# Ending a row norm inside the turn to columns: a product with a diagonal of reciprocal roots on top of a one-row product of the shift

## The chip, the cores and the metric

The kernel runs on one core of one Trainium2 chip. The metric is the device time of one execution in microseconds (us); three runs of the kernel before gave a median of 1448.42 us, with a lowest of 1444.13 and a highest of 1455.28. Names of engines: PE is TensorE, DVE is VectorE, ACT is ScalarE, POOL is GpSimd, SP is SyncE, which here only issues DMAs. PEld is the weight load of PE.

## The reference, cut to what matters

Two layers over 256 tokens of 1024 features, all float32. Layer 0 has two kinds of attention heads and a dense SwiGLU, layer 1 has differential attention and a SwiGLU of 8 experts, of which each token takes two. Every block ends in the same norm:

```
def layer_norm(x, g, b):
    mu = mean(x); var = mean((x - mu)**2)
    return (x - mu) * rsqrt(var + LN_EPS) * g + b

x = layer_norm(ALPHA * x + mixer(x),  ln1_g, ln1_b)
x = layer_norm(ALPHA * x + swiglu(x), ln2_g, ln2_b)

# layer 1, second block
logits = x @ w_router                 # 256 x 8
top_logit, top_e = top_k(logits, 2)
gate = softmax(top_logit)
out[t] = sum over the 2 chosen experts e of gate * swiglu(x[t], w_gate[e], w_up[e], w_down[e])
```

There are four norms: three of them feed products (before the dense SwiGLU, before layer 1, before the router and the experts), and the fourth gives the output.

## The kernel before

**Tiles.** The rows of x lie in two blocks of 128 tokens (`tb` 0 and 1) by 1024 features. Products need x with features on the partitions, so that each norm is followed by a turn: 8 pieces of 128x128 for each block, two banks of PSUM (the accumulation memory that PE writes) to a block, four pieces in each. ACT copies each bank to `xth` (rounded to the product's format), and DVE writes the rest, bank minus `xth`, to `xtl`. Each weight is split in the same way, by ACT to `whi` and by DVE to `wlo` (`split`, `hi`, `lo`), so a product is three products (lines 506, 507 and 508). The weights come as units of 1 MB. SP loads them in the order of use into slots of `raw`, 7 in the dense part and 14 with the experts, and each slot is loaded again once `wlo` of its unit is written (`lo_rdy`).

**Order.** There is no planner. Each engine's program is written out by hand, and semaphores join them. An expert has 42 units (`EXP_ORDER`): for each of 7 columns of hidden features two gate units, two up units, and then two down units of the column before. At unit j, ACT and DVE split unit j + 3, so that three units lie split ahead of PE.

**A norm** (`norm`, `norm_sum`, `norm_end` of DVE, `norm_root` of ACT, `turn` of PE). For each block DVE adds ALPHA times x and the branch's sum out of PSUM into `acc` (line 1384), takes the negated mean (1371), and writes (acc - mean) * gain to x (1395). Beside it, ACT squares with accumulation (995) and takes the root (990). DVE takes the reciprocal (1398) and ends the rows, x * reciprocal root + shift, in two halves (1400). PE turns the finished x by transposes against the identity (535, with the router 780), four to a bank. Between the blocks PE runs `keep_warm`, products of the identity with itself that nobody reads (513): 12 of them in the first two norms. ACT's copy is line 977, DVE's rest line 1259.

**The route.** After the third norm PE forms the router's logits from `xth` and `xtl` (768). DVE picks the two best experts of each token (lines 1512 to 1525), block after block. PE sums the choices into positions (799 to 805), and DVE makes the one-hot matrix `ohot_t` of the first expert (1534). The rows of the first expert are gathered by products with it (816), of `xrh` and `xrl`, the split of the finished x: ACT writes the one (1007), POOL the other (477). ACT also writes `acc`, ALPHA * x (1151), and zeroes `y` (1155).

**The last expert.** Before its first unit, DVE works out the gates and the rows of each token's two outputs (`gates_and_rows`, lines 1643 to 1663, each of these instructions waiting for the one before it). The outputs of all other experts lie in DRAM (`y_rows`). POOL gathers four blocks of 128 rows from there by indirect DMAs (485), and DVE adds them up with their gates (`picked_sum`, 1594) at the units in `PICK_AT`, (18, 23, 28, 33). The first sum waits for all four.

## Time and profile before

| | |
|---|---|
| three runs, us | 1444.13, 1448.42, 1455.28 (median 1448.42) |
| the profiled execution, us | 1446.74, of which span 1444.9 |
| busy in the span | PE 97%, PEld 84%, DVE 77%, ACT 65%, POOL 3% |
| PE's mean granted clock | 0.988 |
| a split of a unit | ACT 1.92, DVE 2.29 us |
| DVE in the slices of the dense SwiGLU (131 to 314 us) | busy 5 to 6 tenths |
| the three norms with a turn | about 118 to 131, 313 to 327, 441 to 454 us |
| the route | about 450 to 472 us |
| the experts | about 472 to 1431 us, one each 119.3 us; the last from 1306.6 us |

The span runs from the first to the last instruction. Matmuls overlap in the records, so that a busy PE may still be waiting for the array. A product of plain float32 operands shows as two records; a transpose, and a product in the rounded format, as one. The granted clock is given as a share of 2.4 GHz: 1.00 is that, 0.50 is 1.2 GHz.

### The profile page before, as it was taken

What the parts mean: (1) busy time and instruction counts of PE and PEld (TensorE: products, weight loads), DVE (VectorE), ACT (ScalarE), POOL (GpSimd) and SP (SyncE); (2) the same over time, 40 slices, a digit from 0 to 9 for tenths busy, and PEclk for the clock granted to TensorE, in tenths of its full rate; (3) what the DMA queues carried; (4) which work ended last, traced back from release to release, by engine and by line L of the source; (5) the groups of instructions that cost most, each with busy time, mean ns of one, the idle gap of its engine ahead of it and who ended that gap; (6) DMA issues with size and microseconds to landing.
All of it is one profiled execution on the core that took longest, in us unless ns stands there. A gap on an engine that the chain in (4) does not pass through costs nothing.

```text
span 1444.9 us, 19906 instructions
## 1 busy us (share of the span) xinstructions
PE 1405.6 (97%) x7580; PEld 1209.9 (84%) x7580; DVE 1118.8 (77%) x978; ACT 945.1 (65%) x838; POOL 41.0 (3%) x30
## 2 busy tenths in 40 slices
PE   8999999999988999999999999999999999998996
PEld 8988999989977888888888888888888888887885
DVE  4646454465566888888888988888888888888897
ACT  4655434445554777777777777777777777776775
POOL 1000000000001000000000000000000000002000
PEclk9999999999997999999999999999999999999998
DMA  9515555544136999999999999999999999998960
GB/s 362 222 64 203 191 185 181 199 146 175 60 161 251 413 384 369 366 402 370 342 411 383 374 364 389 389 357 392 368 357 405 376 367 378 392 372 334 421 235 31
DMA packets 62789, 438.59 MB, mean 304 GB/s; under 512 B 7096, under 2 KB 7120, under 8 KB 11152
## 3 DMA queue, kind: packets, MB, share of 16 engines
q1 hardware_dynamic: 59904, 425.75, 76.7%
q0 software_dynamic: 2688, 11.85, 2.3%
q8 instruction: 36, 0.59, 0.2%
q10 hardware_dynamic: 144, 0.27, 0.1%
q14 instruction: 17, 0.14, 0.0%
HBM read 431.54 MB, written 6.30 MB: 303 GB/s over the span
## 4 chain that ended last, share of the span: by engine, by line
PE 91%; DVE 5%; ACT 2%; issue 1%; DMA 1%; SPq 0%; DVEq 0%; ACTq 0%
PE ps L506 29%; PE ps L508 28%; PE ps L507 28%; PE ps L878 2%; ACT raw L1014 1%; DMA raw<-w_dense 1%; DVE raw L1271 1%; PE ps L664 1%; PE ps L612 1%; DVE acc L1384 1%; ACT biasb L995 1%; DVE wlo L1243 0%; PE ps L836 0%; DVE x L1400 0%; DVE raw L1312 0%
## 5 line engine op out<-in xcount | busy, mean ns | idle before, releaser
L1243 DVE TENSOR_TENSOR wlo<-raw,whi 128x2048 fp32r<-128x2048 f32 x398 | 910.2, 2291 | 207.2 <-ACT whi L962 205.5
L962 ACT ACTIVATE whi<-raw 128x2048 fp32r<-128x2048 f32 x398 | 762.2, 1918 | 273.1 <-PE ps L508 270.4
L506 PE MATMUL ps<-whi,xth 128*128 128x512 f32 (+1 forms) x1144 | 441.5, 386 | 7.5 <-DVE wlo L1243 3.8
L508 PE MATMUL ps<-whi,xtl 128*128 128x512 f32 (+1 forms) x1144 | 434.7, 380 | 0.0
L507 PE MATMUL ps<-wlo,xth 128*128 128x512 f32 (+1 forms) x1144 | 434.4, 380 | 0.0
L506 PEld LDWEIGHTS ps<-whi,xth 128*128 128x128 f32 x1144 | 215.6, 188 | 50.8 <-DVE wlo L1243 6.9
L508 PEld LDWEIGHTS ps<-whi,xtl 128*128 128x128 f32 x1144 | 215.6, 188 | 41.4
L507 PEld LDWEIGHTS ps<-wlo,xth 128*128 128x128 f32 x1144 | 215.9, 189 | 38.6
L506 PE MATMUL ps<-whi,hth 128*128 128x512 f32 x464 | 182.5, 393 | 0.0
L508 PE MATMUL ps<-whi,htl 128*128 128x512 f32 x464 | 180.8, 390 | 0.0
L507 PE MATMUL ps<-wlo,hth 128*128 128x512 f32 x464 | 180.7, 389 | 0.0
L506 PE MATMUL ps<-xth,whi 128*128 128x256 f32 x592 | 169.6, 287 | 3.6 <-issue 3.6
L507 PE MATMUL ps<-xtl,whi 128*128 128x256 f32 x592 | 168.9, 285 | 0.0
L508 PE MATMUL ps<-xth,wlo 128*128 128x256 f32 x592 | 168.8, 285 | 0.0
L506 PEld LDWEIGHTS ps<-xth,whi 128*128 128x128 f32 x592 | 115.0, 194 | 5.1 <-issue 4.5
L507 PEld LDWEIGHTS ps<-xtl,whi 128*128 128x128 f32 x592 | 115.0, 194 | 0.3
L508 PEld LDWEIGHTS ps<-xth,wlo 128*128 128x128 f32 x592 | 115.0, 194 | 0.0
L508 PEld LDWEIGHTS ps<-whi,htl 128*128 128x128 f32 x464 | 87.1, 188 | 18.6
L506 PEld LDWEIGHTS ps<-whi,hth 128*128 128x128 f32 x464 | 87.2, 188 | 18.0 <-issue 0.3
L507 PEld LDWEIGHTS ps<-wlo,hth 128*128 128x128 f32 x464 | 87.2, 188 | 17.3
L471 POOL DMA_INDIRECT biasb<-x_rows,slot_tok x7 | 19.2, 2741 | 744.2 <-DVE slot_tok L1621 744.2
L1582 DVE TENSOR_TENSOR htmp<-htmp,ps 128x512 f32<-128x512 f32 x56 | 38.1, 681 | 0.0
(238 smaller groups left out, 694.4 us busy)
## 6 DMA issues: line engine op xcount, KB each, us to landing
raw<-w_moe SPq DMA_DIRECT2D x336, 1024.0 KB, 7.1
raw<-w_dense SPq DMA_DIRECT2D x62, 1024.0 KB, 4.8
raw<-vec_rows POOLq DMA_DIRECT2D x4, 1024.0 KB, 6.9
y_rows<-work SPq DMA_DIRECT2D x8, 512.0 KB, 8.3
x<-x_in SPq DMA_DIRECT2D x2, 512.0 KB, 5.1
raw<-w_dense SPq DMA_DIRECT2D x2, 512.0 KB, 10.0
raw<-cum_rows POOLq DMA_DIRECT2D x1, 1024.0 KB, 6.9
x_rows<-x SPq DMA_DIRECT2D x2, 512.0 KB, 3.2
```

What stands on the lines that cost most here:

```text
L471: pool.indirect_dma_start(out=xg, out_offset=None, in_=x_rows[:, :], in_offset=bass.IndirectOffsetOnAxis(ap=slot_tok[:, 0:1], axis=0), bou ...
L506: mm(o, lh, rh, start=start, stop=False)
L507: mm(o, lh, rl, start=False, stop=False)
L508: return mm(o, ll, rh, start=False, stop=stop)
L612: r = mm(bank[:, c0:c0 + nk], q, kk, start=True, stop=True)
L664: r = mm(o, PT[g][:, kt, h * P:(h + 1) * P], v, start=kt == 0, stop=kt == qblk)
L878: r = pe.transpose(ps[4][:, i * P:(i + 1) * P], htmp[:, i * P:(i + 1) * P], ident)
L962: A(unit(whi, j), raw[:, slot * UNIT:(slot + 1) * UNIT], ACT.Copy).then_inc(hi_rdy, 1)
L995: link(A(spare[:, 1024:2048], acc[:, tb, :], ACT.Square, bias=st[:, 3:4], accum_out=st[:, 4:5]))
L1014: A(S[g % 2][:, h, 0:nk], S[g % 2][:, h, 0:nk], ACT.Exp, bias=negm[:, g % 2, h:h + 1], accum_out=sm[:, g % 4, h:h + 1]).then_inc(e_rdy, 1)
L1243: dve.tensor_tensor(unit(wlo, j), raw[:, slot * UNIT:(slot + 1) * UNIT], unit(whi, j).bitcast(F32), ALU.subtract).then_inc(lo_rdy, 1)
L1582: dve.tensor_tensor(htmp[:, :], htmp[:, :], ps[2 + c % 2][:, :], ALU.mult).then_inc(m_h, 1)
```

## The change

Three norms no longer write their finished rows ahead of the turn. What DVE leaves in x is (acc - mean) * gain, and beside it `diag`, the identity times the reciprocal root, 128x128. PE first writes the shift into the banks by products of one row (the shift, one partition) with a row of ones (`shift_rows`), and then adds the turned x by products with `diag` (`turn_scaled`). The rows themselves are finished later (`norm_rows`). In the third norm ACT copies the first block before it squares the second.

The first gather uses x itself and the one-hot times the reciprocal root, again on top of one-row products of the shift, in four parts; `xrh` and `xrl` are gone, with POOL's two instructions. POOL zeroes `y` in place of ACT. SP loads slot m = 6 and writes `x_rows` after the slots m = 7 to 13, no longer before them. `gates_and_rows` is cut into seven steps, run at units 1, 3, 6, 8, 12, 14 and 18 of the last expert; ACT's ALPHA * x moves to its unit 6; and `PICK_AT` becomes (24, 27, 30, 33). The counts of `keep_warm` are other ones.

```diff
-WARM_START, WARM_FIRST, WARM_NORM, WARM_HEADS = 9, 7, 12, 2
-WARM_ROUTE = (8, 3, 4, 3, 8)
+WARM_START, WARM_FIRST, WARM_NORM, WARM_HEADS = 9, 7, 9, 2
+WARM_ROUTE = (5, 10, 3, 8)
-PICK_AT = (18, 23, 28, 33)
+PICK_AT = (24, 27, 30, 33)
+ROWS_AT = (1, 3, 6, 8, 12, 14, 18)
+        diag = work[:, 0:TB * P].rearrange("p (t n) -> p t n", t=TB)
...
+            for m in range(DENSE_SLOTS, SLOTS):
+                sp.wait_ge(lo_rdy, N_DENSE + m - 2 * DENSE_SLOTS + 1)
+                load(w_moe[m], moe_slot(m)[0])
+            sp.wait_ge(src_rdy, 8)
+            load(w_moe[DENSE_SLOTS - 1], moe_slot(DENSE_SLOTS - 1)[0])
+            for tb in range(TB):
+                sp.dma_start(x_rows[tb * P:(tb + 1) * P, :], x[:, tb, :]).then_inc(xr_out, 16)
...
-            for tb in range(TB):
-                pool.wait_ge(xr_hi, tb + 1)
-                pool.tensor_tensor(xrl[:, tb, :], x[:, tb, :], xrh[:, tb, :].bitcast(F32), ALU.subtract).then_inc(xr_lo, 1)
+            pool.wait_ge(xt_ps, 4 * 6)
+            pool.memset(y, 0.0).then_inc(ye_rdy, 1)
...
+            def shift_rows(n, tb):
+                if tb == 0:
+                    pe.wait_ge(gb_in, 16 * (n + 1))
+                for kt in range(KT):
+                    mm(ps[2 * tb + kt // 4][:, (kt % 4) * P:(kt % 4) * P + P], gb_extra[0:1, 1, kt * P:(kt + 1) * P],
+                       ones[0:1, :], start=kt % 4 == 0, stop=False)
+            def turn_scaled(n, tb):
+                pe.wait_ge(dg_rdy, 2 * n + tb + 1)
+                for half in range(2):
+                    for i in range(4):
+                        kt = 4 * half + i
+                        r = mm(ps[2 * tb + half][:, i * P:(i + 1) * P], x[:, tb, kt * P:(kt + 1) * P], diag[:, tb, :],
+                               start=False, stop=i == 3)
+                    r.then_inc(xt_ps, 1)
+            def turn_normed(n):
+                for tb in range(TB):
+                    shift_rows(n, tb)
+                    if tb == 1:
+                        keep_warm(WARM_NORM, 5)
+                    turn_scaled(n, tb)
+                turned(n + 2, 3)
...
-            turn(2)
+            turn_normed(0)
-            turn(3)
+            turn_normed(1)
...
             pe.wait_ge(wr_l, 1)
-            keep_warm(WARM_ROUTE[0], 3)
-            turn_router(0)
-            keep_warm(WARM_ROUTE[1], 3)
+            shift_rows(2, 0)
+            turn_scaled(2, 0)
+            shift_rows(2, 1)
             pe.wait_ge(xth_rdy, 4 * 5 + 2)
             logits(0, xth)
-            turn_router(1)
+            keep_warm(WARM_ROUTE[0], 5)
+            turn_scaled(2, 1)
...
# DVE: the end of a block's norm
                 link(dve.reciprocal(std[:, tb, 0:1], std[:, tb, 0:1]))
-                for c, done in ((slice(0, 512), x_half), (slice(512, D), src_rdy)):
-                    dve.scalar_tensor_tensor(out=x[:, tb, c], in0=x[:, tb, c], scalar=std[:, tb, 0:1],
-                                             in1=gb[:, 1, c], op0=ALU.mult, op1=ALU.add).then_inc(done, 1)
+                dve.tensor_scalar(diag[:, tb, :], ident, std[:, tb, 0:1], None, ALU.mult).then_inc(dg_rdy, 1)
+            def norm_rows():
+                for tb in range(TB):
+                    dve.scalar_tensor_tensor(out=x[:, tb, :], in0=x[:, tb, :], scalar=std[:, tb, 0:1],
+                                             in1=gb_extra[:, 1, :], op0=ALU.mult, op1=ALU.add).then_inc(src_rdy, 1)
...
                 turned(t)
                 if k < N_DENSE - 1:
                     split(k - 1 + SPLIT_AHEAD)
+                    norm_rows()
...
             def expert(e, last=False, again=False):
                 for j, (what, c, half) in enumerate(EXP_ORDER):
+                    if last and j in ROWS_AT:
+                        gates_and_rows(ROWS_AT.index(j))
                     if last and j in PICK_AT:
                         picked_sum(PICK_AT.index(j))
...
-            gates_and_rows()
             expert(N_EXP - 1, True)
```

On PE, at the first norm, the kernel before has these rows between the last down product of the branch (lines 506 to 508) and the first product of the next unit. `con` holds the identity.

```order
598 L508 MATMUL ps<-whi,xtl 128x512
599 L535 MATMUL ps<-con,x 128x128 x8
600 L513 MATMUL ps<-con 128x128 x12
601 L535 MATMUL ps<-con,x 128x128 x8
602 L506 MATMUL ps<-xth,whi 128x256
```

The changed kernel has these at the same place. Line 519 is `shift_rows`, 512 `keep_warm`, and 528 `turn_scaled`, with `diag` lying in `work`.

```order
598 L507 MATMUL ps<-whi,xtl 128x512
599 L519 MATMUL ps<-con,raw 128x128 x8
600 L528 MATMUL ps<-work,x 128x128 x8
601 L519 MATMUL ps<-con,raw 128x128 x8
602 L512 MATMUL ps<-con 128x128 x9
603 L528 MATMUL ps<-work,x 128x128 x8
604 L505 MATMUL ps<-xth,whi 128x256
```

The 16 transposes have become 16 products with `diag`, 16 one-row products have come, and 3 of the 12 idle products are gone.

On DVE, in the last expert, the changed kernel has this from the last step of `gates_and_rows` (lines 1689 to 1692, which ends with the rows to pick being known) to the first sum of a picked block (1613). Line 1256 is the split of a unit, 1601 and 1606 are steps of the hidden features.

```order
505 L1689 TENSOR_TENSOR biasb<-biasb 128x16
506 L1690 TENSOR_REDUCE biasb<-biasb 128x2
507 L1691 CAST mx<-biasb 128x2
508 L1692 COPY rec<-biasb 128x2
509 L1256 TENSOR_TENSOR wlo<-raw,whi 128x2048 x2
510 L1601 TENSOR_TENSOR htmp<-htmp,ps 128x512
511 L1256 TENSOR_TENSOR wlo<-raw,whi 128x2048 x4
512 L1606 TENSOR_TENSOR htl<-ps,hth 128x512
513 L1613 SCALAR_TENSOR_TENSOR acc<-biasb,rec,acc 128x1024
```

The kernel before has this between the same two (1663 is the last of its step, 1594 the first sum).

```order
489 L1663 COPY rec<-biasb 128x2
490 L1243 TENSOR_TENSOR wlo<-raw,whi 128x2048 x4
491 L1582 TENSOR_TENSOR htmp<-htmp,ps 128x512
492 L1243 TENSOR_TENSOR wlo<-raw,whi 128x2048 x2
493 L1587 TENSOR_TENSOR htl<-ps,hth 128x512
494 L1243 TENSOR_TENSOR wlo<-raw,whi 128x2048 x2
495 L1582 TENSOR_TENSOR htmp<-htmp,ps 128x512
496 L1243 TENSOR_TENSOR wlo<-raw,whi 128x2048 x4
497 L1587 TENSOR_TENSOR htl<-ps,hth 128x512
498 L1243 TENSOR_TENSOR wlo<-raw,whi 128x2048 x2
499 L1582 TENSOR_TENSOR htmp<-htmp,ps 128x512
500 L1243 TENSOR_TENSOR wlo<-raw,whi 128x2048 x4
```

After these, one step of the hidden features stands before the sum. Between knowing the rows and the first sum there were 18 splits, and now there are 6.

## Rows read from the trace of the kernel before

**Rows 1.** The page's chain that ended last, shares by engine

```profile
PE 91%; DVE 5%; ACT 2%; issue 1%; DMA 1%; SPq 0%; DVEq 0%; ACTq 0%
```

**Rows 2.** Timeline, first norm: start us, length us, engine, line, operation, count

```profile
123.98 1.03 PE L535 MATMUL ps<-con,x 128*128 128x128 f32 x8
...
127.03 1.42 DVE L1400 SCALAR_TENSOR_TENSOR x<-x,std,raw 128x512 f32<-128x512 f32 x2
...
127.84 1.32 PE L535 MATMUL ps<-con,x 128*128 128x128 f32 x8
...
128.36 2.48 DVE L1259 TENSOR_TENSOR xtl<-ps,xth 128x512 fp32r<-128x512 f32 x4
...
128.53 1.26 ACT L977 ACTIVATE xth<-ps 128x512 fp32r<-128x512 f32 x2 [0.83 <-PE ps L535]
...
130.94 0.35 PE L506 MATMUL ps<-xth,whi 128*128 128x256 f32 x1 [1.78 <-issue]
```

**Rows 3.** Stretches of 10 us: length, PE busy, granted clock, DMA share, GB/s

```profile
130.00:140.00 10.00, 9.06 (x63) 0.83 0.79 288
...
320.00:330.00 10.00, 7.91 (x54) 0.84 0.01 2
...
450.00:460.00 10.00, 8.62 (x40) 0.50 0.77 290
460.00:470.00 10.00, 8.22 (x56) 0.67 1.02 430
```

**Rows 4.** Timeline of PE in the attention: products with 128 and with 64 rows

```profile
44.59 1.26 PE L612 MATMUL ps<-raw 64*128 64x128 f32 x16
...
71.91 3.68 PE L664 MATMUL ps<-raw 128*128 128x64 f32 x32
```

**Rows 5.** Timeline of the route, all engines

```profile
444.10 1.95 PE L513 MATMUL ps<-con 128*128 128x128 f32 x16
...
455.60 1.85 PE L768 MATMUL ps<-wrt,xth 128*128 128x16 f32 x8
...
455.90 4.67 POOL L477 TENSOR_TENSOR wlo<-x,whi 128x1024 fp32r<-128x1024 f32 x2 [36.94 <-ACT whi L1007]
...
456.19 2.10 DVE L1513 SCALAR_TENSOR_TENSOR biasb<-biasb,con 128x8 f32<-128x8 f32 x1
...
461.64 0.17 DVE L1519 TENSOR_REDUCE biasb<-ps 128x8 f32<-128x16 f32 x1
...
463.62 0.23 DVE L1525 SCALAR_TENSOR_TENSOR biasb<-biasb 128x8 f32<-128x8 f32 x1
...
464.50 0.43 PE L803 MATMUL ps<-biasb,con 128*128 128x8 f32 x2
...
466.34 1.24 PE L816 MATMUL ps<-ohot_t,whi 128*128 128x128 f32 x8
...
471.85 0.48 PE L506 MATMUL ps<-whi,xth 128*128 128x512 f32 x1
```

**Rows 6.** Page, DMA issues: size, median us from issue to landing

```profile
raw<-w_moe SPq DMA_DIRECT2D x336, 1024.0 KB, 7.1
```

**Rows 7.** Chain in order of time: one same step in the last three experts

```profile
1178.08 0.44 PE ps L878 x4
...
1297.37 0.44 PE ps L878 x4
...
1422.53 0.44 PE ps L878 x4
```

**Rows 8.** Timeline of the last expert: first sum on DVE, first and last gather on POOL

```profile
1327.10 1.86 POOL L485 DMA_INDIRECT biasb<-y_rows,mx  x1 [103.15 <-DMA y_rows<-work]
...
1334.75 3.09 POOL L485 DMA_INDIRECT work<-y_rows,mx  x1 [0.30 <-issue]
...
1367.91 1.28 DVE L1594 SCALAR_TENSOR_TENSOR acc<-biasb,rec,acc 128x1024 f32<-128x1024 f32 x1
```

**Rows 9.** The four gathers (line 485), issue to landing

```profile
DMA to landing us min/median/max: 10.2/12.3/13.8
```

More of the change, by code:

```diff
@@ L423, in store @@
                 for tb in range(TB):
-                    for c, done, before in ((slice(0, 512), x_half, 6), (slice(512, D), src_rdy, 8)):
+                    for c, done, before in ((slice(0, 512), x_half, 0), (slice(512, D), src_rdy, 8)):
                         sp.wait_ge(done, before + 2 * n + tb + 1)
@@ L674, in mix @@
                               first and r2 == 0, last and r2 == 1)
-                    if last and tb == 1 and i == 1:
+                    if last and i == 1:
                         r.then_inc(y_left, 1)
@@ L805, in _ @@
             mm(ps[7][0:1, 0:8], ones[:, 0:1], chosen[:, 1, :], start=False, stop=True).then_inc(cnt_ps, 1)
-            keep_warm(WARM_ROUTE[3], 5)
+            keep_warm(WARM_ROUTE[2], 5)
             def first_gather():
+                for kt in range(KT):
+                    mm(ps[kt // 2][:, (kt % 2) * P:(kt % 2) * P + P], gb_extra[0:1, 1, kt * P:(kt + 1) * P],
+                       ones[0:1, :], start=kt % 2 == 0, stop=False)
                 pe.wait_ge(oh_rdy, 1)
-                for q in range(2):
-                    for t, bank, ready in ((xrh, 1 + 2 * q, xr_hi), (xrl, 2 * q, xr_lo)):
-                        pe.wait_ge(ready, TB)
-                        for kt in range(4 * q, 4 * q + 4):
-                            for tb in range(TB):
-                                r = mm(ps[bank][:, (kt % 4) * P:(kt % 4) * P + P], t[:, tb, kt * P:(kt + 1) * P],
-                                       ohot_t[:, tb * P:(tb + 1) * P], start=tb == 0, stop=tb == TB - 1)
-                        if q == 1 and t is xrl:
-                            r.then_inc(ga_ps, 1)
-                        else:
-                            r.then_inc(g0_ps, 1)
+                for q in range(4):
+                    for kt in range(2 * q, 2 * q + 2):
+                        for tb in range(TB):
+                            r = mm(ps[q][:, (kt % 2) * P:(kt % 2) * P + P], x[:, tb, kt * P:(kt + 1) * P],
+                                   ohot[:, tb, :], start=False, stop=tb == TB - 1 and kt % 2 == 1)
+                    if q == 3:
+                        r.then_inc(ga_ps, 1)
+                    else:
+                        r.then_inc(g0_ps, 1)
             def find_rows(n):
@@ L1001, in norm @@
                 norm_root(n, 0)
+                if t == 5:
+                    turned(t, (0, 1))
                 norm_root(n, 1)
-                turned(t)
-                if k == N_DENSE - 1:
-                    for tb in range(TB):
-                        act.wait_ge(src_rdy, 6 + tb + 1)
-                        A(xrh[:, tb, :], x[:, tb, :], ACT.Copy).then_inc(xr_hi, 1)
+                turned(t, (2, 3) if t == 5 else range(4))
                 split(k - 1 + SPLIT_AHEAD)
@@ L1187, in expert @@
                                 "p (k n) -> p k n", k=4), out_bank(nn), ACT.Copy).then_inc(ye_rdy, 1)
+                    if j == 6 and last:
+                        A(acc[:, :, :], x[:, :, :], ACT.Copy, scale=ALPHA).then_inc(acc_rdy, 1)
                     if j < PER_EXP - 3 or not last:
@@ L1200, in expert @@
                         A(stats[:, 1, 5:6], eps[:, 0:1], ACT.Sqrt)
-            for q in range(2):
-                act.wait_ge(g0_ps, 2 * q + 1)
-                r = A(xth[:, 4 * q:4 * q + 4, 0:P], ps[1 + 2 * q][:, :].rearrange("p (k n) -> p k n", k=4), ACT.Copy)
+            for q in range(4):
+                if q < 3:
+                    act.wait_ge(g0_ps, q + 1)
+                else:
+                    act.wait_ge(ga_ps, 1)
+                r = A(xth[:, 2 * q:2 * q + 2, 0:P], ps[q][:, 0:2 * P].rearrange("p (k n) -> p k n", k=2), ACT.Copy)
+                if q < 3:
+                    r.then_inc(g0_hi, 1)
             r.then_inc(ga_hi, 1)
-            act.wait_ge(ga_ps, 1)
-            split(N_DENSE - 1 + SPLIT_AHEAD)
             A(stats[:, 1, 5:6], eps[:, 0:1], ACT.Silu)
```

140 lines of the change are left out of this document (63 added, 77 removed).

## The prediction

> **What bounds the kernel now.** I read the chain of waits first: PE holds 91% of it [rows 1]. Only a stretch in which PE waits, runs at the low clock or does work of no use can therefore give time back, and whatever the change adds to PE there is paid in full. Three kinds of place show in the timeline and in the granted clock: the first two norms, the route, and the start of the last expert. The sum is made against the profiled execution, 1446.74 us (span 1444.9 and 1.8 around it), 1.7 below the median of the three runs.
>
> **First norm.** The last product of the branch is issued just before 123.98, where the first transposes start. The second block's rows are finished in halves from 127.03, the transposes run from 127.84, ACT's two copies take 1.26 us from 128.53, and DVE's four rests run back to back from 128.36 to 130.84. PE goes on at 130.94 [rows 2]. The change takes away the 1.42 us of ending rows in halves. It puts in one 128x128 instruction on DVE, whose price no row has; it is below the 0.71 us of one half. So `diag` is ready at about 127.3 (127.7 at worst), half a microsecond before the first transposes started.
>
> That is not what ends last, though. PE's own row is now 8 one-row products, 8 with `diag`, 8 one-row, 9 idle ones, and then the 8 with `diag` that everything waits for. A plain float32 product is two records. 32 records of 128 rows take 3.68 us with the tail of the last, some 0.27 [rows 4]: 0.11 a record, **0.22 us a product**. A transpose is one record, 0.11: eight take 1.03 with the tail [rows 2]. The price of a one-row product has no row. From above it is 0.22. From below: products with 64 rows take 1.26 us for 16 records, 0.15 a product [rows 4], but they alternate in pairs between the upper and the lower half of the array, so that some can overlap (five slots in place of eight would give 1.1 plus the tail), and ours all use the same row. I take 0.22, since 64 rows are no cheaper once that overlap is counted; 0.15 stays as one bound, and nothing (0) as the other, since no row has one row.
>
> The Trainium skill, in "TensorE: Matmul & The Clock Gate", section "LDWEIGHTS (loading the stationary operand)", says that a 32x128 load takes as long as a 128x128 one, since columns count and not the contraction. By that rule the one-row products save nothing, and the sum stays as it is. It speaks against this change, and no run here shows a single row yet.
>
> So PE reaches the last eight products at 123.98 + 33 x 0.22 = 131.2, four microseconds after `diag` is ready: PE itself has become the bound. They end at 133.0, the last bank is there 0.25 later, ACT's copy takes 0.6, DVE's rest 0.6, and PE goes on at **134.6, 3.7 us later** than before. At 0.15 the 16 one-row products would be 1.1 us cheaper and it would be 133.5 (+2.6); at 0 they would be 3.5 cheaper, 131.1 (+0.2).
>
> **The clock pays some of it back.** After the wait and transposes, the clock fell in both norms: the mean granted clock was 0.83 in the 10 us from 130 and 0.84 in those from 320 [rows 3], so 1.7 us of work were lost each time. Now PE works on plain products until the end of the turn and then waits 1.4 us. I expect the fall to be gone: 3.7 - 1.7 = **+2.0 in each of the two norms, +4.0**; +3.7 each if it stays.
>
> DVE's finished rows, 1.42 a block [rows 2], now come after the turn and one split. Two units lie split there, and the splits of the stretch behind leave DVE a third of its time or more, so that they are hidden; if that cover were gone they would cost 2.8 a norm. The shift is loaded during the branch, together with the gain, as before.
>
> **The route.** Before: the stream ends at 444.10. The clock is at 0.50 all through 450 to 460 and 0.67 from 460 to 470 [rows 3], so that eight logit products take 1.85 us. POOL's two instructions hold from 455.90 to 460.57, and DVE's 128x8 step at 456.19 takes 2.10 instead of the 0.23 at 463.62. The second block's choice runs from 461.64 to 463.85, PE's position products start at 464.50, the gather at 466.34, and the first unit at 471.85 [rows 5].
>
> After, at full clock: 24 products from 444.10 to 449.4, 8 logits (0.9) and 5 idle products (1.1) to 451.4, 8 with `diag` to 453.1, three more groups of logits to 455.9. DVE chooses for the first block from about 454.6, when its last rest is written, and for both in 2 x 2.2 us, to 459.0, with nothing of POOL in its way. PE's 10 idle products from 457.3 end at 459.5. That is 5.0 before 464.50. From there to the gather stood 1.84; now 0.6 of position products, 3 idle and 8 one-row products stand there, 3.0. The gather (16 plain products, 3.5, as the 32 rounded ones before) starts at 462.5 and, with 8 idle products as before, the first unit at 467.8: **-4.1**. But narrow logit products did not bring the clock back before, from 450 to 459 at 0.50, and now a run of them and a wait of 1 us stand from 453.1 to 457. I count one fall of the clock, 1.7: **-2.4**. Bounds: -4.1 without it, and 0 if the whole route stays at 0.50.
>
> POOL now zeroes `y` at about 453.4. No row has that; between 0 and the 2.35 of one of its instructions before, on DVE's path. I take 0, since the 0.5 us by which PE's idle products outlast DVE covers a part, and keep +1.8 (2.35 - 0.5) for the range.
>
> The Trainium skill, in "SBUF — State Buffer", section "SBUF: two separate sides", says that DVE and GpSimd share a pair of ports by an exclusive lock for a whole instruction. The 2.10 us at 456.19 agree with it. By it the zeroing too could hold DVE, up to the bound just given.
>
> SP's loads of m = 7 to 13 no longer wait for the norm; m = 6 does, until DVE has finished the rows at about 472. Its unit comes at 467.8 + 6 x 2.84 = 484.8 (an expert's 119.29 us by 42 units, [rows 7]) and its two splits take four of these, so it has to land by about 480.5; it lands after 7.1 [rows 6], at 479. The 1 us to spare makes this worth nothing; if it took 12 us it would cost 4.
>
> **The last expert.** The same step of the last three experts stands at 1178.08, 1297.37 and 1422.53 [rows 7]: 119.29 and then 125.16, so **5.9 us** were lost to the 24 chained steps ahead of it and to the fall of the clock behind the wait. Each step takes some 0.2 (ten in the 2.2 us from 461.64, [rows 5]). In pieces of three and four, 0.6 to 0.8 us, they are shorter than the sum of 1.28 that stands at 1367.91 between two splits [rows 8], with nothing lost around it. That takes the 5.9 away.
>
> But the rows to pick are now known only at unit 18. Without the 5.9 us, DVE gets there at 1367.91 - 5.9 = 1362.0 [rows 8], and is through at 1362.8. POOL issues the first gather 0.3 later, at 1363.1, and the last 7.65 behind it, as 1334.75 is behind 1327.10, at 1370.8 [rows 8]. That one lands after 10.2 to 13.8 us [rows 9], at 1381.0 to 1384.6. DVE wants it at unit 24, six units of 2.84 after unit 18: at 1379.0. It waits 2.0 to 5.6 us. Of DVE's lead the sum itself (1.28) takes all, and the next sums come at every third unit, so that nothing is made up. With the median landing, 12.3, PE stands for 4.1 us, and the clock falls behind such a wait (1.7): 5.8. **Net -0.1**, between -2.2 and +1.4.
>
> **Sum.** +4.0 - 2.4 - 0.1 = +1.5: 1446.74 + 1.5 = **1448.2 us**, which is no change.
>
> **Rivals.**
> - *The one-row products cost next to nothing.* For: no row of the trace has one; the idle products are fewer by three. Against: 64 rows show no saving beyond overlap. Norms 0 (or -3.4 with the clock kept), the route another 3.2 better (16 one-row products less on its path, of which the choice hides some), last expert as above: -5.7 to -9.1, about **1439.5**. Chance 0.12.
> - *The picked rows are there in time*, because the gathers now meet queues that are less behind than after the stall. For: before, they ran while the loads caught up. Against: even the shortest landing, 10.2, is 2.0 late. Then the last expert gives its 5.9: +4.0 - 2.4 - 5.9 = -4.3, **1442.5**. Chance 0.15.
> - *Slower: the clock doesn't hold through the turn*, because products of one row count for little as work, as the narrow logits seem to. Then the norms' 41 products run in part at twice the price. Each fall costs 1.7; two more in each norm and the old one kept make 2 x (3.7 + 3.4) = 14.2. The route stays at 0.50 and gives nothing; the last expert -0.1: +14, **1461**. It decides as soon as the granted clock is 0.50 anywhere between 124 and 134. Against: half of these products are full ones of the kind that held the clock before. Chance 0.08.
> - *The change doesn't do what it says for the route*: m = 6 lands late (12 us), or the zeroing holds DVE: +2 to +6, **1452**. Chance 0.10.
>
> The forecast itself has 0.55, with its own range of 1444 to 1452. The range for 8 in 10 reaches down to the two faster cases and leaves out the clock: 1439 to 1455. A measurement of this kernel can tell about 1%, 14 us, from no change. Faster by over that needs both faster rivals at once with the clock kept: 0.06. Slower by over that is the third rival at its full price: 0.05. Within: 0.89.
>
> **What would show it.** In the first norm PE should be busy from 124 to 133 with no wait for DVE, reach its last eight products at about 131, and go on at 134 to 135, at clock 1.00 from 130 to 140. If one-row products take under 0.15 us each, the first rival holds. In the route, DVE's 128x8 steps should all take 0.2, and the first unit should start 24 to 26 us after the last product of the branch, where it was 27.7 (444.10 to 471.85). In the last expert PE should have no wait at unit 3, and one of 2 to 6 us at unit 27, behind a DVE that waits for the gathers. No such wait proves the last expert's term wrong; a clock of 0.50 inside a turn proves the norms' term wrong.

## The result: 1.3% slower, where no change was predicted

The changed kernel takes 1468.63 us (median of four runs, 1462.69 to 1473.94), the kernel before 1450.97 beside it (four runs, 1444.13 to 1455.28): ratio 1.0129, 95% interval 1.0100 to 1.0159. A second set of runs gave 1463.67 against 1448.36, ratio 1.0122 (1.0077 to 1.0166). The prediction of 1448.2 with a range to 1455 was wrong.

The profiled execution took 1467.65 us, with a span of 1465.9; that of before had 1444.9. The difference of 21.0, by the stretches between PE's own landmarks (us; the norms run from PE's first instruction of the turn to the first unit behind it, the route from the last product of the branch to the first unit of the experts, the last expert between the steps of [rows 7]):

| | to first norm | norm | to second | norm | to route | route | to [rows 7] | expert before | last expert | rest |
|---|---|---|---|---|---|---|---|---|---|---|
| before | 123.98 | 6.96 | 188.71 | 7.12 | 117.33 | 27.75 | 706.23 | 119.29 | 125.16 | 22.4 |
| changed | 127.17 | 11.45 | 187.33 | 13.09 | 117.49 | 32.86 | 706.30 | 119.30 | 128.55 | 22.4 |
| difference | +3.2 | +4.5 | -1.4 | +6.0 | +0.2 | +5.1 | +0.1 | 0 | +3.4 | 0 |

The +3.2 stands in code that did not change; in this execution the granted clock fell to 0.50 at 68 us, behind a wait. The second set's profile has no such fall there, reaches the first norm at 124.22, and has all else as here (span 1462.9); so 18 us are the change's.

The chain of waits by engine, where the shares of PE and of DMA rose by a point each and DVE's fell by two [rows 1]:

```profile
PE 92%; DVE 3%; DMA 2%; ACT 2%; issue 1%; POOL 0%; SPq 0%; POOLq 0%; DVEq 0%; ACTq 0%
```

The first norm, in the timeline (start us, length us, engine, line, operation, count, and in brackets the idle time before with what ended it), to be held against [rows 2]:

```profile
127.17 2.05 PE L519 MATMUL ps<-con,raw 1*128 1x128 f32 x16
129.14 2.05 PE L528 MATMUL ps<-work,x 128*128 128x128 f32 x16
...
130.12 0.29 DVE L1412 TENSOR_SCALAR work<-con,std 128x128 f32<-128x128 f32 x1
...
131.12 2.05 PE L519 MATMUL ps<-con,raw 1*128 1x128 f32 x16
...
133.10 2.27 PE L512 MATMUL ps<-con 128*128 128x128 f32 x18
...
135.21 1.95 PE L528 MATMUL ps<-work,x 128*128 128x128 f32 x16
...
138.62 0.36 PE L505 MATMUL ps<-xth,whi 128*128 128x256 f32 x1 [1.46 <-ACT xth L990]
```

L519 is the shift's one-row products, L528 those with the diagonal, L512 the idle ones; each product is two records. The second block's diagonal is written at 130.4, and PE gets to the last eight products 4.8 us later, at 135.21: PE sets the end, as predicted. The rows of 16 records follow each other at 1.97 to 1.98 us, 0.247 us a product, the one-row ones and those with the diagonal between them alike.

The second norm is the same program, but takes 1.6 us more. First PE's rows, then stretches of 2 and 10 us (length, busy time of PE, PEld, DVE, ACT and POOL, granted clock, DMA share, GB/s):

```profile
329.91 2.05 PE L519 MATMUL ps<-con,raw 1*128 1x128 f32 x16
331.89 2.98 PE L512 MATMUL ps<-con 128*128 128x128 f32 x18
334.66 2.92 PE L528 MATMUL ps<-work,x 128*128 128x128 f32 x16
339.04 0.36 PE L505 MATMUL ps<-xth,whi 128*128 128x256 f32 x1 [1.46 <-ACT xth L990]
```

```profile
130.00:140.00 10.00, 8.54 (x72) 8.14 (x71) 3.51 (x7) 4.59 (x6) 0.00 (x0) 1.00 0.00 1
...
332.00:334.00 2.00, 2.00 (x15) 2.00 (x16) 0.00 (x0) 0.00 (x0) 0.00 (x0) 0.82 0.00 0
334.00:336.00 2.00, 2.00 (x12) 2.00 (x11) 0.00 (x0) 0.00 (x0) 0.00 (x0) 0.50 0.00 0
...
460.00:470.00 10.00, 10.00 (x47) 9.55 (x46) 1.65 (x4) 2.32 (x5) 0.00 (x0) 0.51 0.54 224
```

Behind the first norm the clock holds (1.00 from 130 to 140, where [rows 3] have 0.83). In the second it falls inside the turn, from about 333, though PE has not waited once since the turn began at 325.95; it falls while the full idle products run, right behind the one-row ones. From 460 to 470 it is at 0.51, again with PE busy for all ten microseconds. That is the route, which began at 456.53 [rows 5]:

```profile
456.53 2.05 PE L519 MATMUL ps<-con,raw 1*128 1x128 f32 x16
458.51 2.85 PE L528 MATMUL ps<-work,x 128*128 128x128 f32 x16
461.29 3.78 PE L519 MATMUL ps<-con,raw 1*128 1x128 f32 x16
465.00 1.88 PE L790 MATMUL ps<-wrt,xth 128*128 128x16 f32 x8
466.72 2.48 PE L512 MATMUL ps<-con 128*128 128x128 f32 x10
...
475.34 3.44 PE L512 MATMUL ps<-con 128*128 128x128 f32 x20
...
482.39 5.46 PE L829 MATMUL ps<-work,x 128*128 128x128 f32 x32
...
489.39 0.48 PE L505 MATMUL ps<-whi,xth 128*128 128x512 f32 x1
```

The same 16 one-row records take 1.98 us at 456.53 and 3.71 at 461.29. The clock is low three times in this route: from 459.6 to 469.4, from 476.6 to 480 behind PE's wait of 0.89 for the choice, and from 483.5 to 486.1 inside the gather (L829).

In the last expert, the waits of DVE and of PE (from 1300 to 1450: for what; us in total, times, longest), the step's own row, the landing of the four gathers [rows 9], and the first and the last of their issues [rows 8]:

```profile
DVE acc L1613 <- DMA work<-y_rows,mx: 6.9, 1, 6.9
```

```profile
PE ps L505 <- DVE wlo L1256: 6.9, 1, 6.9
```

```profile
1381.44 2.38 POOL L484 DMA_INDIRECT biasb<-y_rows,mx  x1 [139.88 <-DVE rec L1692]
...
1389.24 2.33 POOL L484 DMA_INDIRECT work<-y_rows,mx  x1 [0.30 <-issue]
```

```profile
DMA to landing us min/median/max: 10.1/11.9/14.4
```

```profile
1403.65 1.28 DVE L1613 SCALAR_TENSOR_TENSOR acc<-biasb,rec,acc 128x1024 f32<-128x1024 f32 x1 [6.90 <-DMA work<-y_rows,mx]
```

The last gather is issued at 1389.24 and is in at 1403.65, 14.4 us later. All four are as slow as before; they start later.

### The profile page after: what moved, and what is told of

It is laid out like the page before. It is cut to its first block, busy times and chain, and to the rows that moved or that the text cites. A ratio compares the mean times of both kernels' runs of the same rounds, so it can differ in the third digit from the quotient of the medians.

```text
span 1465.9 us, 20204 instructions
## 1 busy us (share of the span) xinstructions
PE 1428.4 (97%) x7728; PEld 1231.5 (84%) x7728; DVE 1116.0 (76%) x979; ACT 943.2 (64%) x837; POOL 36.7 (3%) x29
## 4 chain that ended last, share of the span: by engine, by line
PE 92%; DVE 3%; DMA 2%; ACT 2%; issue 1%; POOL 0%; SPq 0%; POOLq 0%; DVEq 0%; ACTq 0%
PE ps L505 28%; PE ps L507 28%; PE ps L506 28%; PE ps L891 2%; DMA work<-y_rows,mx 1%; PE ps L512 1%; PE ps L519 1%; PE ps L528 1%; ACT raw L1025 1%; DMA raw<-w_dense 1%; DVE raw L1284 1%; PE ps L686 1%; PE ps L634 1%; DVE wlo L1256 0%; PE ps L849 0%
## 5 line engine op out<-in xcount | busy, mean ns | idle before, releaser
L1272 DVE TENSOR_TENSOR xtl<-ps,xth 128x512 fp32r<-128x512 f32 x24 | 15.9, 687 | 36.0 <-ACT xth L990 36.0
L990 ACT ACTIVATE xth<-ps 128x512 fp32r<-128x512 f32 x24 | 13.7, 596 | 42.5 <-PE ps L528 24.5
```

The costliest lines, as they stand in the source:

```text
L1272: dve.tensor_tensor(xtl[part], ps[bank][:, :].rearrange("p (k n) -> p k n", k=4), xth[part].bitcast(F32), ALU.subtract).then_inc(xtl_rdy, 1)
```

## Experiments

**The theories.** A: PE's own products ahead of the last eight set the end of a turn, and each costs its time. C: on top of it, one-row products do not hold PE's clock, so that it falls while PE is busy with them. Its rival, M: falls come by the moment at which a stretch begins, whatever PE does. G: the rows to pick are known too late for the gathers of the last expert.

The stretches of each experiment's profile in us, as in the table above (the changed kernel had 11.45, 13.09, 32.86 and 128.55 there, the kernel before 6.96, 7.12, 27.75 and 125.16); a star marks a norm or route in which PE ran products at 0.50:

| | norm | norm | route | last expert | median us | ratio (95%) |
|---|---|---|---|---|---|---|
| 5: changed again | 11.46 | 13.09* | 32.86* | 128.56 | 1463.67 | 1.0122 (1.0077, 1.0166) |
| 1: norms by transposes | 6.95 | 7.10 | 24.92 | 128.36 | 1452.22 | 1.0017 (0.9996, 1.0037) |
| 2: last expert as before | 11.46 | 13.09* | 31.07* | 125.06 | 1459.05 | 1.0062 (1.0038, 1.0086) |
| 3: shift by 128 rows | 10.77 | 10.77 | 25.35* | 127.57 | 1454.73 | 1.0041 (1.0019, 1.0063) |
| 4: no shift products | 7.20 | 7.20 | 22.15* | 127.53 | 1444.00 | 0.9962 (0.9947, 0.9978) |
| 7: choice's rows early | 11.45 | 11.45 | 32.87* | 120.53 | 1454.95 | 1.0047 (1.0033, 1.0061) |
| 10: no idle products in norms | 9.45 | 13.91* | 35.98* | 128.51 | 1464.90 | 1.0115 (1.0069, 1.0162) |
| 8: transposes, rows early | 6.95 | 7.10 | 24.05* | 120.51 | 1439.02 | 0.9937 (0.9914, 0.9960) |
| 11: the same, route filled | 6.97 | 7.10 | 21.62* | 120.54 | 1438.23 | 0.9919 (0.9895, 0.9944) |
| 12: transposes, route 128 rows | 6.96 | 7.10 | 26.99* | 120.56 | 1441.74 | 0.9950 (0.9929, 0.9970) |

The numbers in front are those of the experiments below, whose edits are shown against the changed kernel, cut to what matters. Each row's stretches come from one profile. The kernel before took 1449.48 beside 1 to 4, 1448.36 beside 5, 7 and 8, and 1449.96 beside 10 to 12.

**1. The first two norms by transposes, the rest as changed.**

```diff
-            turn_normed(0)
+            turn(2)
...
-            turn_normed(1)
+            turn(3)
...
-                    norm_scale(n, tb, roots)
+                    (norm_end if n in [0, 1] else norm_scale)(n, tb, roots)
```

> The changed kernel with the first two norms as before: rows finished on DVE, 16 transposes and 12 idle products on PE. Theory A (PE's plain products stand ahead of the last eight and set the end of the turn): first norm from its first PE product after the branch to the next unit 11.4 us in the changed kernel, 7.0 here; the second 13.0 there, 7.1 here; less 1.5 us each where the clock falls again behind the turn. 7 to 8 us faster than the changed kernel, so 8 to 13 us slower than before. Theory B (the norms only look long, and the loss is that the rows' finishing behind the turn delays the splits of the branch that follows): the units of the dense SwiGLU would start closer together here than in the changed kernel, and the turn would be no shorter.

By the ratios 15 to 16 us came back, twice what theory A alone allows. The norms are at 6.95 and 7.10, so A is right about them. The expectation's theory B is out: between the norms lie 188.7 us here as in the kernel before, and 187.3 in the changed kernel, so finishing the rows behind the turn delayed nothing there. The route, unchanged from the changed kernel, takes 24.92 in place of 32.86: in this profile the clock is 1.00 all through it.

```profile
446.00:452.00 6.00, 6.00 (x47) 5.33 (x46) 3.74 (x9) 2.44 (x6) 0.00 (x0) 1.00 1.01 421
452.00:462.00 10.00, 9.11 (x80) 8.90 (x79) 6.25 (x24) 6.63 (x8) 0.95 (x1) 1.00 0.54 224
462.00:472.00 10.00, 10.00 (x89) 9.70 (x89) 6.11 (x15) 3.44 (x8) 0.00 (x0) 1.00 0.01 2
```

The gather, 5.46 us in the changed kernel, takes:

```profile
466.39 3.84 PE L833 MATMUL ps<-work,x 128*128 128x128 f32 x32
```

So at the full clock the route is 2.8 us shorter than before, where -4.1 had been worked out, and 7.9 us of the changed kernel's route are the clock's. How much of the 2.8 is itself the clock's, since the kernel before had 0.50 in much of its route [rows 3], no run separates. It also speaks for a part of M: the same route with the same 24 one-row products lets the clock fall in one execution and not in another.

**2. The last expert as before, the rest as changed.**

```diff
-PICK_AT = (24, 27, 30, 33)
-ROWS_AT = (1, 3, 6, 8, 12, 14, 18)
+PICK_AT = (18, 23, 28, 33)
+ROWS_AT = ()
...
+            for step in range(7):
+                gates_and_rows(step)
             expert(N_EXP - 1, True)
```

> The changed kernel with all of gates_and_rows ahead of the last expert's first unit and the sums at units 18, 23, 28 and 33 as before. Theory A (the four gathers start only at unit 18 and land after the first sum wants them): the last expert loses 5.9 us as before in place of 9.3, so 3.4 us faster than the changed kernel; PE's wait of 6.9 us behind unit 26 goes and one of 3.8 us at unit 3 comes. Theory B (the sums at every third unit are too close for DVE): then the wait would have to be spread over units 27 to 36, and the same 3 us come back through the wider spacing, with no single wait on the gathers in the changed kernel to take away.

The last expert takes 125.06, 3.5 less than in the changed kernel, as expected. PE's wait of 6.9 is gone, one of 3.8 near its start is back, and no waits were spread over the later units, so the expectation's theory B is out. The time is lower by more (1.0062, where the changed kernel has 1.0129 and 1.0122). The profile puts the rest on stretches that this edit does not touch: 1.8 less in the route, no fall on the way to it (115.93 in place of 117.49), and 1.9 less ahead of the first norm.

**3. The shift's products over 128 rows**: all partitions hold the shift, the other operand is 1/128 everywhere; as many products, with the same result.

```diff
-gb_extra[0:1, 1, kt * P:(kt + 1) * P], ones[0:1, :],
+gb_extra[:, 1, kt * P:(kt + 1) * P], share,
...
+            dve.memset(share, 1.0 / P)
```

> The changed kernel with each one-row product replaced by one of 128 rows (the shift's row stands in all partitions, and the row of ones is a 128x128 matrix of 1/128): the same sum, the same number of instructions. Theory A1 (rows don't matter to a product's time): 16 records in 1.98 us as with one row. Theory C (one-row products do not count as work for the clock): the granted clock stays at 1.00 in the second norm (0.83 over 10 us in the changed kernel) and from the third norm to 462, so some 1.5 to 5 us faster than the changed kernel. If only the time of the products mattered, the clock would fall at the same places and the time would be the same.

It is 0.8 to 0.9% faster than with one row (1.0041, where the changed kernel has 1.0129 and 1.0122), some 12 us, where 1.5 to 5 had been expected. The mean granted clock was 0.985 to 0.994 in its twelve executions and 0.979 to 0.987 in the eight of the changed kernel. The second norm:

```profile
323.68 1.95 PE L520 MATMUL ps<-ohot_t,raw 128*128 128x128 f32 x16
325.46 1.95 PE L529 MATMUL ps<-work,x 128*128 128x128 f32 x16
327.24 1.95 PE L520 MATMUL ps<-ohot_t,raw 128*128 128x128 f32 x16
329.03 2.17 PE L513 MATMUL ps<-con 128*128 128x128 f32 x18
331.04 1.95 PE L529 MATMUL ps<-work,x 128*128 128x128 f32 x16
334.45 0.35 PE L506 MATMUL ps<-xth,whi 128*128 128x256 f32 x1 [1.46 <-ACT xth L991]
```

No fall in either norm, nor in the route up to PE's wait for the choice, and 16 records in 1.78 us, not 1.98: 0.223 us a product, the price that the prediction took. In this turn one row is dearer than 128, for itself and for the products with the diagonal beside it.

**4. No shift products.** The output lacks the shift of the first three norms. The gather's one-row products are gone too.

```diff
-                for kt in range(KT):
-                    mm(ps[2 * tb + kt // 4][...], gb_extra[0:1, 1, kt * P:(kt + 1) * P],
-                       ones[0:1, :], start=kt % 4 == 0, stop=False)
...
-                               start=False, stop=i == 3)
+                               start=i == 0, stop=i == 3)
```

> The changed kernel without any product of the shift (the turned x and the first gather lack the shift): 16 products less in each norm and 8 less in the gather. Theory A: PE reaches the last eight products 3.9 us earlier in each of the first two norms, at 127.2 + 4.1 = 131.3 in place of 135.2 by the first norm's times, a microsecond after the diagonal is ready, so the turn ends 3.9 earlier; the third norm 2 to 4 earlier, the gather 2: 11 to 14 us faster than the changed kernel together with the clock that they cost. If one-row products were hidden or free, nothing would move.

Each norm takes 7.20: 4.25 less than 11.45 for 16 products less, 0.27 each (0.247 of their own, and the others are back at 0.223). This is theory A at its plainest, and it shows how little the diagonal could bring here: without any shift, the turn is still 0.2 longer than by transposes (6.96). In all it is 23 to 24 us faster than the changed kernel by the ratios, where 11 to 14 had been expected; by the profile 10.7 of that lie in the route and 5.9 in the second norm, where the falls of the turn and of the route ahead of the choice are gone as well.

**5. The changed kernel again**, on the same chip as all later numbers.

> The changed kernel once more, beside the next ones on one chip. Both theories: 1.010 to 1.016 of the kernel before. Clock theory (one-row products do not hold TensorE's clock): the granted clock falls to 0.50 inside the second norm's turn again, between the start of the one-row products and the last product with the diagonal (13.1 us to the next unit), and in the route while the one-row products run. Rival (the falls come by the moment at which the stretch happens to begin, whatever PE does): the second norm's turn may show no fall, and then takes 11.4 us as the first.

Norms 11.46 and 13.09, route 32.86, last expert 128.56: all four as in the first profile to 0.01 us. The clock theory expected this. It doesn't rule the moment out, though: number 7, the same program up to the last expert, begins its second norm at 322.81 where this one begins at 323.00, and its clock does not fall there (18 idle records in 2.11 us, where this one takes 2.78):

```profile
328.74 2.27 PE L512 MATMUL ps<-con 128*128 128x128 f32 x18
330.85 1.95 PE L528 MATMUL ps<-work,x 128*128 128x128 f32 x16
```

**6. 96 idle products with one row, and 96 with 128**, in the turns of number 3, which had no fall. One execution was taken, as of number 9.

```diff
                         keep_warm(WARM_NORM, 5)
+                        for _ in range(96):
+                            if n == 0:
+                                mm(ps[5][:, 0:P], ident[0:1, :], ident[0:1, :], start=True, stop=True)
+                            else:
+                                mm(ps[5][:, 0:P], ident, ident, start=True, stop=True)
```

> All shift products with 128 equal rows, and two blocks of 96 idle products each: with one row in the first norm's turn, with 128 rows in the second's, both behind full 128-row products at clock 1.00. Clock theory: the first block starts at 0.124 us a record, the granted clock falls to 0.50 inside it, and the rest takes about 0.22 a record, 30 to 40 us in all; the second takes 192 x 0.11 = 21 us at 1.00 throughout. Rival (by the moment alone): no more of the low clock in one than in the other; 24 and 21 us. A third way, in which a one-row product is simply slower and nothing else: 24 us at 1.00 for the first.

The two blocks in the timeline, and the clock in stretches of the one and of the other:

```profile
132.68 37.47 PE L541 MATMUL ps<-con 1*128 1x128 f32 x192
...
369.93 21.60 PE L543 MATMUL ps<-con 128*128 128x128 f32 x192
```

```profile
134.00:136.00 2.00, 2.00 (x20) 2.00 (x19) 0.00 (x0) 0.00 (x0) 0.00 (x0) 1.00 0.00 0
136.00:138.00 2.00, 2.00 (x16) 2.00 (x15) 0.00 (x0) 0.00 (x0) 0.00 (x0) 0.74 0.04 8
138.00:140.00 2.00, 2.00 (x11) 2.00 (x11) 0.00 (x0) 0.00 (x0) 0.00 (x0) 0.50 0.00 0
...
168.00:170.00 2.00, 2.00 (x11) 1.85 (x9) 0.00 (x0) 0.00 (x0) 0.00 (x0) 0.50 0.00 0
...
370.00:380.00 10.00, 10.00 (x92) 10.00 (x92) 0.00 (x0) 0.00 (x0) 0.00 (x0) 1.00 0.00 0
380.00:390.00 10.00, 10.00 (x92) 10.00 (x91) 0.00 (x0) 0.00 (x0) 0.00 (x0) 1.00 0.01 2
```

PE is busy without a gap in both. Under one-row products the clock is at 0.50 from 138 on and stays there up to 170, where full products come again; under 128 rows it never leaves 1.00. Theory C is shown for a long row of them, and M falls as the whole cause. The place in the program is no rival: in number 9 the clock holds at the first place and falls at the second. In the changed kernel's turn, where 25 of the 41 products are full ones, C alone does not decide: the first norm never fell, and the second fell in three of four profiles (number 5). There the moment has a part.

**7. The pieces of the choice at units 0 to 8 of the last expert.**

```diff
-ROWS_AT = (1, 3, 6, 8, 12, 14, 18)
+ROWS_AT = (0, 1, 2, 3, 4, 6, 8)
```

> The seven pieces of the choice stand at units 0, 1, 2, 3, 4, 6 and 8 of the last expert, where the changed kernel has them at 1 to 18; all else as changed. Theory (the rows to pick, known at unit 18, leave the gathers 17 us, and the slowest landed after 18): the gathers are in before unit 24, DVE and PE have no wait there, and the last expert's step comes 119.3 to 120.5 us after the one before, where it was 128.6: -8 against the changed kernel. Rival (the waits move: pieces close together delay the splits of the first units, as the 24 steps in one chain did before): PE waits 3 to 6 us near units 3 to 8, -2 to -5. Second rival (the gathers land late because of the loads that they meet): still 3 to 7 us of waiting at unit 24, 0.

The last expert takes 120.53, -8.0 against the changed kernel and -4.6 against before; PE has no wait in it. The gathers took as long to land (10.5 to 14.9 us). They were first issued at 1348.26, 39.6 us after the step of [rows 7] in the expert before the last, where the changed kernel issued at 66.5:

```profile
1348.26 2.38 POOL L484 DMA_INDIRECT biasb<-y_rows,mx  x1 [113.05 <-DVE rec L1692]
```

Theory G is shown, and pieces closer together delayed nothing that PE waited for.

**8. All three norms by transposes, rows early, and POOL's splits still out of the route.** The main lines:

```diff
-            shift_rows(2, 0)
-            turn_scaled(2, 0)
-            shift_rows(2, 1)
+            keep_warm(8, 3)
+            turn_router(0)
...
-            turn_scaled(2, 1)
+            turn_router(1)
...
-WARM_ROUTE = (5, 10, 3, 8)
+WARM_ROUTE = (3, 4, 3, 8)
...
-ROWS_AT = (1, 3, 6, 8, 12, 14, 18)
+ROWS_AT = (0, 1, 2, 3, 4, 6, 8)
```

> All three norms end by finished rows and transposes, as in the kernel before (no diagonal, no shift products); the choice's pieces at units 0 to 8; GpSimd's two splits stay out of the route, which has 3, 4, 3 and 8 idle products. Theory: the norms as before (0), the route 20 to 23 us to the first unit in place of 27.75 (-5 to -8), the last expert 119.3 to 120.5 in place of 125.2 (-5 to -6): -10 to -14, ratio 0.990 to 0.993 to the kernel before. Rival (the route's gain came from the diagonal): route 27 us and clock low, -5, 0.9965.

0.63% faster than before, just short of what was expected (0.990 to 0.993). The route takes 24.05, longer than the 20 to 23 expected, as the clock is at 0.50 for most of it (456 to 468), with waits of 0.7 us and narrow products ahead of that. It is still 3.7 shorter than before and 0.9 shorter than number 1's at the full clock: its gain did not need the diagonal.

**9. The same two blocks with 64 rows, and with 128 rows but 16 columns**, against number 6:

```diff
-                                mm(ps[5][:, 0:P], ident[0:1, :], ident[0:1, :], start=True, stop=True)
+                                mm(ps[5][:, 0:P], ident[0:64, :], ident[0:64, :], start=True, stop=True)
-                                mm(ps[5][:, 0:P], ident, ident, start=True, stop=True)
+                                mm(ps[5][:, 0:16], ident, ident[:, 0:16], start=True, stop=True)
```

> As the kernel with 96 idle products of each kind, but with 64 rows in the first norm's turn, and with 128 rows and only 16 columns out (the shape of the logits) in the second's. There one row fell to 0.50 3.8 us after its start, and 128 rows of 128 columns stayed at 1.00. Theory, rows used count: 64 rows fall too, later than one row did or only in part; the narrow ones keep all rows busy and hold the clock, so that the falls of the route come from its one-row products and waits. Rival, work in a time counts: 64 rows fall, and so do the narrow ones, since their moving columns are an eighth. Third: only very few rows fall, both hold.

```profile
132.97 21.70 PE L541 MATMUL ps<-con 64*128 64x128 f32 x192
...
352.71 37.43 PE L543 MATMUL ps<-con 128*128 128x16 f32 x192
```

```profile
132.00:140.00 8.00, 8.00 (x73) 7.88 (x71) 0.00 (x0) 0.00 (x0) 0.00 (x0) 1.00 0.01 2
140.00:150.00 10.00, 10.00 (x92) 10.00 (x91) 0.00 (x0) 0.00 (x0) 0.00 (x0) 1.00 0.00 0
...
356.00:358.00 2.00, 2.00 (x15) 2.00 (x14) 0.00 (x0) 0.00 (x0) 0.00 (x0) 0.65 0.00 0
358.00:360.00 2.00, 2.00 (x11) 2.00 (x11) 0.00 (x0) 0.00 (x0) 0.00 (x0) 0.50 0.00 0
```

64 rows hold the clock and cost what 128 do (21.70 us for 96 products, 21.60 in number 6). Sixteen columns lose it about as soon as one row does. The logits have that shape. None of the three expectations had it right: rows alone don't decide, since the narrow ones use all 128, and 64 rows do not fall.

**10. No idle products in the two norms** (`WARM_NORM` 0 in place of 9).

> The 9 idle products of the two norms' turns are gone; all else as changed. Theory (PE's own products ahead of the last eight set the end of the turn, the diagonal is ready 5 us before): each turn 2.0 us shorter at the full clock, 9.4 where it was 11.45, -4.0 in all; where the clock falls more, 13.1 to at most 12, -2. Rival (the idle products hold the clock up): the fall comes in both turns and eats it, 0 to +2.

Nothing in the time (1.0115). The first norm got its 2.0 us (9.45). In the second the clock fell from 323 on, earlier than with the idle products, and it takes 13.91; the route, whose code did not change, takes 35.98. Both expectations held in part. That the idle products held the clock up is likely for the second norm but rests on one profile, and number 7 shows that this turn's fall varies by itself.

**11. Number 8 with more idle products in the route**, against number 8:

```diff
-WARM_ROUTE = (3, 4, 3, 8)
+WARM_ROUTE = (6, 8, 3, 8)
...
             turn_router(0)
+            keep_warm(3, 5)
```

> The version with transposes and early rows, and in the route more idle products where TensorE waited: 3 after the first block's transposes, 6 in place of 3 behind the first logits, 8 in place of 4 in the choice. Theory (the clock fell at 456 in that route because of the waits of 0.7 us around narrow logits): the clock holds, route 20.5 to 22.5 us in place of 24.05, -2 to -3, ratio to before 0.991 to 0.993. Rival (the narrow products themselves let it fall): still 0.50 from there, 24 to 25 us, ratio 0.994 to 0.995.

The best version: 1438.23 us, 0.8% faster than before and 2.0 to 2.1% faster than the changed kernel by the ratios. None of its three norms has a diagonal. The route is at 21.62, with one fall left, in 458 to 461, where PE has just waited for the choice.

**12. Norms by transposes, the route as changed with 128 rows for the shift, rows early.**

> First two norms by finished rows and transposes, the third and the first gather as changed but with the shift's products over 128 equal rows, choice's pieces at units 0 to 8. Theory: norms 0, route 23.7 to 25.4 us (-2.4 to -4.0 from 27.75), last expert -4.6: -7 to -9, ratio 0.994 to 0.995. Rival (the diagonal holds the clock better in the route than transposes do): route under 23, ratio 0.992 or less, below that of the version with transposes throughout.

0.5% faster than before, as expected, behind number 11. The route missed its range (26.99, where 23.7 to 25.4 was expected): the clock fell behind the wait of 0.89 for the choice, and the 20 idle records there took 4.6 us, where they take 2.5 at the full clock of number 1.

## Why the prediction was wrong, by its own steps

- **Bound by PE; the norm's turn ends with PE's own products.** Right, and the largest term of the sum stood on it. The price was off: 0.247 us for a one-row product and for each product with the diagonal between them, where 0.22 was taken. In the norm that made 4.5 of 3.7. The 0.22 was read from a row of [rows 4] whose products are only 64 columns wide; the idle ones of 128 columns in [rows 5], 16 records in 1.95 us with the tail, would have given the same, and number 3 has 0.223. The Trainium skill, in "TensorE: Matmul & The Clock Gate", "LDWEIGHTS (loading the stationary operand)", says that a weight load of fewer rows takes as long, and the trace agrees: 96 products took 21.60 us with 128 rows and 21.70 with 64, and one row was no cheaper. The first rival, that they cost next to nothing, is gone.
- **"The clock pays some of it back."** This step failed. The fall behind the first norm went (-1.4 of -1.7). In the second it moved into the turn (+1.6). Behind that turn some 1.4 came back too, as numbers 2 and 7 show (115.9 us to the route, where the kernel before has 117.33), but here a fall at 428 to 436 in unchanged code took it again (+0.2). The reason given, that PE now works on plain products until the end, took any product for work that holds the clock. Numbers 3 and 6 show that products of one row do not hold it.
- **The route, -2.4.** The same failure, at its largest: +5.1, 7.5 off. At the full clock it takes 24.92, -2.8 (number 1), near the figure; one fall of 1.7 was counted, and the falls cost 7.9. The bound of 0 for "the whole route at 0.50" was no bound: the kernel before paid for its low clock on fewer products, while now a row of 8 shift products, parts of those with the diagonal, logits, idle products and a part of the gather run at half the clock. The prediction had seen that narrow products do not bring the clock back, and number 9 shows it: 0.50 to the end of their row.
- **The last expert, -0.1.** The mechanism was right (no wait at unit 3, one of DVE at unit 24 and of PE behind it), its size was not: 6.9 us of wait, where 2.0 to 5.6 had been bounded and 4.1 taken, so that the stretch came out at +3.4. The first gather starts 0.8 us after the rows are known, not 0.3, and the last one, which all wait for, took the longest to land, 14.4 and not the median 12.3. A sum over several transfers that must all be in goes by the slowest.
- **The zeroing on POOL, the load of m = 6.** Right at nothing. POOL's zeroing takes 0.95 us at 471.40 and DVE's instruction beside it its usual 0.69; from the route to [rows 7] the difference is 0.1. Without POOL's splits DVE's 128x8 steps take 0.2, as predicted.
- **The rivals.** The third, slower by the clock, had 1461 and 0.08. It was the right mechanism. Its own sign, 0.50 between 124 and 134, did not come (1.00 there); the general sign that the prediction ends on, 0.50 inside a turn, did in the second norm. It took too much for the norms (14.2, where they made 9.3 by the profile) and nothing for the route and the last expert, so that its 1461 is near by a part of luck. It was put down because "half of these products are full ones", which was enough in the first norm, and in the second only in number 7. The kernel had a hint that deserved more than 0.08: logits at 0.50 with PE busy from 450.5 to 459 [rows 3, 5].

By these steps the 21.0 are 4.5 - 1.4 and 6.0 + 0.2 for the norms, 5.1, 3.4, and 3.3 in code that did not change.

**What stays open.** Why the clock fell inside the second norm in three profiles of the changed turn and not in number 7, and never in the first, though all run the same products; between numbers 5 and 7 only the moment differs, between the norms also what PE did before. Why one-row products in the turn, and the full ones between them, lie 0.124 us a record apart, while the one-row records of number 6 before the fall lie 0.111 apart (the 11th starts at 133.90, the 28th at 135.80), as full ones do. So a one-row product costs what a full one does when it runs among its like, and both cost more in the mix. And the fall between 428 and 436 in unchanged code, behind a short wait of PE, which both profiles of the changed kernel have and no other.

## What to carry to other kernels

Count a product twice: its time (a float32 product with one row cost as much as one with 128, or more), and whether it holds the clock. If a one-row product must stand on the path, try it with full rows, as in number 3, where that cost nothing. Full products mixed in did not save the second norm. Look at more than one profile before a fall of the clock is called a property of the program. When work is moved later to free its old place, ask at once by when its result is needed and count back from the slowest of its transfers.

## What the runs showed of the hardware

- A gapless row of 96 float32 products with one row (1x128 on 128), or with 16 columns (128x16), let the granted clock fall from 1.00 to 0.50 (2.4 to 1.2 GHz); the same number with 64 or with 128 rows held it (one profile each, numbers 6 and 9). The Trainium skill, in "TensorE: Matmul & The Clock Gate", "HAM oscillation — how this bites in real kernels", tells of falls behind waits; these fell with PE busy at 100%.
- A full-clock turn of 41 products took 0.68 us more with one-row shift products than with 128-row ones (11.45 against 10.77).
- Four indirect gathers in a row landed 10.1 to 14.9 us after their issue while expert weights streamed (10.2 to 13.8 before, 10.1 to 14.4 changed, 10.5 to 14.9 in number 7).
